# Depthwise convolution in a two-layer backbone step: one tap per channel tile moved from TensorE to VectorE, the first VectorE tap moved to ScalarE, and a later place for the low part of the gated input

## What is computed

```python
def conformer_conv(h, w_pw1, b_pw1, w_dw, b_dw, ln_g, ln_b, w_pw2, b_pw2):
    a = h @ w_pw1 + b_pw1                                  # 1024 -> 2048 channels
    g = a[..., :D_MODEL] * jax.nn.sigmoid(a[..., D_MODEL:])
    y = depthwise_conv(g, w_dw, width 31, padding 15) + b_dw
    y = jax.nn.silu(layer_norm(y, ln_g, ln_b))
    return y @ w_pw2 + b_pw2
```

## Time and profile before

| | |
|---|---|
| Median of three runs | 1706.77 us (1700.06 to 1707.30) |
| The profiled execution, its own time | 1705.06 us |
| Its span in the profile | 1703.1 us |
| TensorE matmuls / VectorE / ScalarE / GpSimd, busy in the whole span | 97% / 56% / 37% / 14% |
| Mean granted TensorE clock | 0.988 of full speed |
| The stretch that the change touches | about 957 to 1144 us in the span |

### The profile page before, as it was taken

How to read it: one execution, slowest core, us unless ns; L and a number is a source line. 1 busy time by engine, 2 the same in 40 slices (tenths; PEclk the granted TensorE clock), 3 DMA queues, 4 the chain that set the end, 5 groups by cost and what they waited for, 6 DMA issues and landing times.

```text
span 1703.1 us, 26511 instructions
## 1 busy us (share of the span) xinstructions
PE 1650.8 (97%) x11277; PEld 1599.8 (94%) x11277; DVE 958.4 (56%) x1617; ACT 636.5 (37%) x988; POOL 242.1 (14%) x288
## 2 busy tenths in 40 slices
PE   8989999989999999999999999999999999999998
PEld 6988778789999999999999999999999999999998
DVE  5556666565774645454458899996663223223222
ACT  3435545453543423342336434354342211221112
POOL 0001111000164523452343000001000000000000
PEclk9999999999999999999999999999999999999999
DMA  8222232142253434433342111010222222221211
GB/s 309 94 68 81 81 94 71 33 137 75 90 164 118 154 97 130 158 125 120 116 124 81 50 50 51 25 50 1 75 77 73 82 67 87 70 89 54 93 56 63
DMA packets 131709, 154.74 MB, mean 91 GB/s; under 512 B 11809, under 2 KB 115177, under 8 KB 131592
## 3 DMA queue, kind: packets, MB, share of 16 engines
q1 hardware_dynamic: 117824, 109.68, 20.4%
q0 software_dynamic: 13440, 43.26, 8.1%
q10 hardware_dynamic: 328, 0.10, 0.0%
HBM read 148.93 MB, written 2.79 MB: 89 GB/s over the span
## 4 chain that ended last, share of the span: by engine, by line
PE 67%; DVE 12%; ACT 2%; issue 2%; POOL 1%; DMA 0%; DVEq 0%; ACTq 0%; POOLq 0%
PE PS L605 21%; PE PS L607 21%; PE PS L610 21%; DVE YACC L2124 7%; PE PS L674 1%; ACT WH L1168 1%; POOL BGACC L582 1%; DVE SUM L1585 1%; PE PS L701 1%; PE PS L927 1%; DVE WL L1577 1%; DVE GP L2103 0%; DVE Y L2133 0%; PE PS L890 0%; DVE Y L2156 0%
## 5 line engine op out<-in xcount | busy, mean ns | idle before, releaser
L605 PE MATMUL PS<-HH,WH 128*128 128x320 f32 x1776 | 412.8, 314 | 11.7 <-DVE HL L1725 4.4
L607 PE MATMUL PS<-HL,WH 128*128 128x320 f32 x1776 | 406.8, 311 | 0.0
L610 PE MATMUL PS<-HH,WL 128*128 128x320 f32 x1776 | 405.7, 310 | 0.0
L1577 DVE TENSOR_TENSOR WL<-RAW,WH 128x2048 fp32r<-128x2048 f32 (+2 forms) x95 | 214.4, 2257 | 204.4 <-ACT WH L1168 203.8
L605 PEld LDWEIGHTS PS<-HH,WH 128*128 128x128 f32 x1776 | 298.0, 190 | 16.0 <-issue 5.7
L607 PEld LDWEIGHTS PS<-HL,WH 128*128 128x128 f32 x1776 | 300.5, 190 | 0.0
L610 PEld LDWEIGHTS PS<-HH,WL 128*128 128x128 f32 x1776 | 300.2, 190 | 0.0
L1168 ACT ACTIVATE WH<-RAW 128x2048 fp32r<-128x2048 f32 (+2 forms) x95 | 171.7, 1807 | 116.6 <-PE PS L610 116.6
L1741 DVE SCALAR_TENSOR_TENSOR X<-PS,MODV,X 128x128 f32<-128x128 f32 (+2 forms) x192 | 72.4, 433 | 206.6 <-PE PS L610 206.6
L582 POOL TENSOR_TENSOR BGACC<-BGACC,BGW 128x512 f32<-128x512 f32 x98 | 134.9, 1376 | 207.1 <-ACT BGW L1423 206.0
L605 PE MATMUL PS<-HIDH,WH 128*128 128x320 f32 x704 | 162.3, 312 | 1.0 <-DVE HIDL L2061 0.7
(11 more groups left out here) (293 smaller groups left out, 2306.4 us busy)
## 6 DMA issues: line engine op xcount, KB each, us to landing
BGW<-in_w_mod POOLq DMA_DIRECT2D x112, 256.0 KB, 3.0
RAW<-in_ffn_w_gate SPq DMA_DIRECT2D x22, 1024.0 KB, 5.3
RAW<-in_ffn_w_up SPq DMA_DIRECT2D x22, 1024.0 KB, 5.3
RAW<-in_ffn_w_down SPq DMA_DIRECT2D x16, 1024.0 KB, 5.1
MODA<-in_w_mod POOLq DMA_DIRECT2D x48, 256.0 KB, 4.0
MODS<-in_w_mod SPq DMA_DIRECT2D x16, 512.0 KB, 12.1
RAW<-in_conv_w_pw SPq DMA_DIRECT2D x16, 512.0 KB, 4.9
RAW<-in_ffn_w_down SPq DMA_DIRECT2D x8, 768.0 KB, 4.4
```

The lines of the kernel that those rows point to most:

```text
L605: mm(o, wh, xh, start=first, stop=False)
L607: mm(o, wh, xl, start=False, stop=False)
L610: ins = mm(o, wl, xh, start=False, stop=last)
L1577: V.tensor_tensor(WL[:, u % 2, 0:n], RAW[:, u % 2, 0:n], WH[:, u % 2, 0:n].bitcast(F32), ALU.subtract).then_inc(lo_done, 1)
```

## The change

The first VectorE tap with the bias becomes a ScalarE instruction behind the GPH copy; tiles 0 to 6 have one tap fewer on TensorE (10, and 12 for tile 6) and so one more off it; tile 7 keeps 18. VectorE waits for ScalarE's tap before its own first one. `gated` no longer has any tap nor GPL in it; GPL is made by `gated_low`, which stands behind all taps of the iteration. `cut` is 19 for tiles 1 to 5 (two taps stand behind `gated(i+1)`), 12 for tile 0 and 8 for tile 6 as before.

```diff
-PE_TAPS = (11, 11, 11, 11, 11, 11, 13, 18)
+PE_TAPS = (10, 10, 10, 10, 10, 10, 12, 18)
...
                 A(GPH[i % 2][:], GP[i % 2][:], ACT.Copy).then_inc(sem("gp_hi"), 1)
+                j = PE_TAPS[i]
+                A(YACC[i % 2][:], GP[i % 2][:, j:j + RUN], ACT.Identity, scale=WTAP[:, i, j:j + 1],
+                  bias=VT2[:, V2["b_dw"] + i:V2["b_dw"] + i + 1]).then_inc(sem("tap_first"), 1)
...
                     was_read(dve, n)
-                first_tap(i)
-                taps(i, 1, 2)
+
+            def gated_low(i):
+
                 dve.wait_ge(sem("gp_hi"), i + 1)
                 V.tensor_tensor(GPL[i % 2][:], GP[i % 2][:], GPH[i % 2][:].bitcast(F32), ALU.subtract).then_inc(sem("gp_lo"), 1)
...
-            def first_tap(i):
-
-                j = PE_TAPS[i]
-                link(V.tensor_scalar(YACC[i % 2][:], GP[i % 2][:, j:j + RUN], WTAP[:, i, j:j + 1],
-                                     VT2[:, V2["b_dw"] + i:V2["b_dw"] + i + 1], ALU.mult, ALU.add))
-
             def taps(i, first, end):
 
                 acc, g = YACC[i % 2], GP[i % 2]
                 j0 = PE_TAPS[i]
+                if first == 1:
+                    dve.wait_ge(sem("tap_first"), i + 1)
                 for j in range(j0 + first, min(j0 + end, TAPS)):
...
             gated(0)
+            gated_low(0)
             for i in range(KT):
                 split_units(U[("glu", i)] + 2)
                 if i:
                     joined(i - 1)
 
-                cut = 8 if i == KT - 2 else 12 if i == 0 else TAPS
-                taps(i, 2, cut)
+                cut = 8 if i == KT - 2 else 12 if i == 0 else TAPS - PE_TAPS[i] - 2
+                taps(i, 1, cut)
                 if i + 1 < KT:
                     gated(i + 1)
                 taps(i, cut, TAPS)
+                if i + 1 < KT:
+                    gated_low(i + 1)
             joined(KT - 1)
```

## The result

The changed kernel took 1715.79 us (median of 8 runs, 1709.47 to 1718.28), the kernel before, run beside it and with its earlier runs, 1704.76 us (8 runs, 1700.06 to 1709.74). The ratio is 1.006 with a 95% interval of 1.0043 to 1.0076: slower by 0.6%. The profiled execution's span is 1713.5 us against 1703.1.

The account below looks back on a forecast made before the run. VectorE was taken to bound the convolution. Its longer tiles, the late GPL(7), 2.3 us of clock loss and 2.84 us of clock holders put the mean +10.45 us later: 1705.06 becomes 1715.5 us, range 1709 to 1719.

Parts of the forecast that it names:

- VectorE sets the pace: Convolution stretch: VectorE's list, 24.56 us a tile before, sets the time, so TensorE's 6.35 us taken away buy nothing.
- The tap on ScalarE: Between ScalarE's copy and rounding: VectorE's low weight part starts 0.72 us later per tile, bounds 0.14 and 0.82.
- The rule that such work belongs on VectorE: Skill's advice against the ScalarE tap, 0.62 us on VectorE against 0.82; by the rule alone 1.6 us in sum.
- TensorE as the most contended engine: Skill's pick by share of weight loads, 94%; the forecast said the chain of the convolution stretch does not agree.
- What a tile costs TensorE: Convolution tile on TensorE: 24.3 us before the change against VectorE's 24.56, then 23.4 against 25.3.
- the rival with TensorE: Convolution: TensorE sets the pace, so the change takes 6.35 us off, 1698.7 us; chance 0.05.
- Late GPL(7): Iteration 6: eleven taps ahead of GPL(7) leave TensorE idle 6.5 to 8 us, so cv(7) ends last.
- The nine taps in tile 0: Tile 0: nine taps ahead of GPL(1); any wait of cv(1) comes out of TensorE's 5 us wait ahead of b(3).
- The clock: At cv(7), behind TensorE's idle time: the granted clock falls and costs 2.3 us, bounds 1.7 and 4.8.
- The clock holders: Behind cv(7): the holders' 2.84 us end last, against VectorE's 1.72 for joining and sum.
- TensorE's waits ahead of b(i+1): Each tile: TensorE waits nearly 2 us (1 to 2) for the gated input, about 5 us in tile 2.
- All behind the mean moves with it: Behind the mean: one dependent chain, shifted by the same +10.45 us as the mean.

Follow-up runs that it names:

- e4_taps_only: Kernel before with only the changed kernel's tap shares, one tap per tile from TensorE to VectorE in tiles 0 to 6: 1713.06 us, ratio 1.0048.
- e5_first_tap_only: Changed kernel with the old tap shares, ScalarE's first tap behind the weight unit's rounding, GPL two taps behind the gated input in every tile: 1696.82 us, ratio 0.9956.
- e1_low_early: Changed kernel with GPL of tile 7 made two taps behind its gated input instead of eleven: 1711.33 us, ratio 1.003.
- e2_hold_cv7: Changed kernel with 26 more matmuls without use ahead of TensorE's wait for GPL(7), to keep the clock up: 1710.09 us, ratio 1.0035.
- e6_no_holders: Changed kernel without the 12 clock holders ahead of the mean: 1717.36 us, ratio 1.0076 to the kernel before.
- e9_tile7_19: e5_first_tap_only with 19 instead of 18 taps of tile 7 on TensorE: 1698.73 us, ratio 0.9969 to the kernel before.
- e8_scalar_tap_first: e5_first_tap_only with ScalarE's tap ahead of the rounding, as in the changed kernel: 1704.60 us, ratio 1.0002 to the kernel before.

## Why the prediction was right

The forecast was 1715.5 us, slower by more than 0.5%; measured were 1715.79 and a ratio of 1.006. Step by step, all counted from the start of the first gated input:

| step | forecast | measured |
|---|---|---|
| gated(1) | 16.95 | 17.06 |
| gated(2) | 47.25 | 47.37 |
| gated(6) | 148.40 | 148.95 |
| gated(7) | 163.40 | 164.04 |
| start of GPL(7) | 174.87 | 175.52 |
| start of cv(7) | 175.8 | 176.50 |
| cv(7) longer by the clock | 2.3 | 2.43 |
| the mean | 197.3 | 197.94 |

- **VectorE sets the pace:** shown by e4_taps_only, where TensorE's 6.35 us bought nothing and VectorE's 6.55 were paid in full.
- **The tap on ScalarE:** its mechanism was right, its size somewhat off. I took 0.72 us from the rows of Identity with a bias; the tap takes 0.92 us in itself (0.82 estimated) and 0.83 from start to start, just past my upper bound of 0.82. Six rounding waits at 0.11 more are the 0.64 by which gated(7) came later. The new instruction has a scale from memory beside the bias, which those rows lacked; whether this makes the 0.10 was not tried.
- **The rule that such work belongs on VectorE** (the Trainium skill, "ScalarE: Activation LUTs", Rules for kernel authors): e5_first_tap_only measured 4.79 us of gain for the opposite. The instruction is indeed longer on ScalarE, 0.92 against 0.62 us, and that costs nothing where that engine is idle and nobody waits behind it.
- **TensorE as the most contended engine** (the Trainium skill, "Perfetto Trace Analysis", Identifying the Most-Contended Engine), at 94% by weight loads: in this stretch not so, by e4_taps_only.
- **What a tile costs TensorE:** counted too high. The working from the end gave 24.3 us before the change; from the start of one tile's convolution to the next it is 24.05 to 24.07 us in tiles 3 to 5. The margin to VectorE's 24.56 was 0.5 us and not 0.24, which makes the rival with TensorE weaker and changes no term of the sum.
- **Late GPL(7):** right, 4.57 us by e1_low_early, the clock's share in it. The nine taps in tile 0 made TensorE wait 1.27 us ahead of cv(1), inside its time to spare, as forecast. The idle time of 6.62 us lies at the lower end of my 6.5 to 8, as the clock had fallen ahead of b(7).
- **The clock:** 2.3 forecast, 2.43 measured, 2.35 by e2_hold_cv7. The size was borrowed from another stretch, so that it came this near is partly luck.
- **The clock holders:** they do end last, but by 0.45 us (e6_no_holders); the forecast's 2.84 against 1.72 made it 1.12.
- **TensorE's waits ahead of b(i+1):** 4.57 us in tile 2 (about 5 forecast), then 0.43, 1.98, 0.43, 1.99 where I had 1 to 2 in each. They alternate. Behind 1.98 the clock fell and the slow matmuls used up most of the next wait; behind 0.43 it stayed up. The five stretches behind the waits of 4.57, 0.43, 1.98, 0.43 and 1.99 us, in order:

```profile
1003.70:1008.50 4.80, 4.79 (x22) 4.79 (x23) 4.04 (x4) 4.80 (x9) 0.00 (x0) 0.64 0.02 3
1029.10:1033.50 4.40, 4.39 (x30) 4.39 (x31) 3.64 (x4) 4.40 (x7) 0.00 (x0) 1.00 0.01 2
1054.50:1059.00 4.50, 4.50 (x20) 4.50 (x21) 3.74 (x4) 4.50 (x8) 0.00 (x0) 0.62 0.00 0
1079.90:1084.50 4.60, 4.60 (x31) 4.60 (x32) 3.83 (x4) 4.60 (x8) 0.00 (x0) 1.00 0.00 0
1105.30:1110.00 4.70, 4.70 (x21) 4.70 (x22) 3.94 (x4) 4.70 (x8) 0.00 (x0) 0.64 0.00 0
```

- **"All behind the mean moves with it"** was wrong by 1.73 us in the profiled run. The sum is close partly by chance: the span of the profiled execution grew by 10.4 us, which is +11.08 in M, +1.73 behind it, and -2.33 for a first gated input that came earlier, within what it moves by between like kernels. Up to the mean the forecast had +10.45 us where 11.08 were measured.

## What to carry to other kernels

Ask who waits for the next instruction on the helping engine. Work moved onto an idle engine is free only behind the things that others wait for: here the same ScalarE instruction cost all it saved ahead of the rounding, and won 4.8 us behind it. When a producer step moves behind other work, check it in each iteration of the loop, the irregular last ones above all: two taps behind it were harmless in five tiles, eleven in one tile cost 4.6 us.

## What the runs showed of the hardware that was not expected

The stretch of light work behind the mean (single-column matmuls, clock holders, small VectorE steps) has a length of 22.77 us in e5_first_tap_only, 24.98 before, 26.71 in the changed kernel and 26.81 in e9_tile7_19, with the same instructions. It goes with the granted clock: over all eleven profiles it is 22.77 us at a mean clock of 0.93, 24.98 to 25.34 at 0.80, and 26.02 to 26.81 at 0.74 to 0.76. These are that stretch before, then in e5_first_tap_only, then in e9_tile7_19 (PEclk 0.80, 0.93 and 0.75):

```profile
1144.30:1169.30 25.00, 22.79 (x150) 22.11 (x151) 12.12 (x33) 8.88 (x13) 6.12 (x4) 0.80 0.00 1
```

```profile
1140.40:1163.20 22.80, 19.83 (x151) 18.97 (x151) 12.14 (x33) 8.94 (x13) 6.13 (x4) 0.93 0.00 1
```

```profile
1137.40:1164.20 26.80, 24.41 (x151) 23.74 (x151) 12.10 (x33) 8.91 (x13) 6.12 (x4) 0.75 0.00 1
```

In the changed kernel the clock stayed at its lower level for 13.6 us on end here, though TensorE was busy all the time:

```profile
1161.00:1174.60 13.60, 13.60 (x65) 13.60 (x66) 3.26 (x18) 1.56 (x3) 3.07 (x2) 0.50 0.00 1
```

The other surprise is that the length of an idle time of about 2 us does not tell whether the clock falls behind it. In e4_taps_only TensorE stood for 2.08 us ahead of b(5) and 2.09 ahead of b(6); behind the first the clock stayed up, behind the second it fell:

```profile
1056.60:1061.00 4.40, 4.40 (x30) 4.40 (x31) 4.18 (x4) 4.40 (x9) 0.00 (x0) 1.00 0.00 0
1082.10:1086.50 4.40, 4.39 (x21) 4.39 (x22) 4.18 (x4) 4.40 (x9) 0.00 (x0) 0.67 0.00 0
```

In e6_no_holders it stood for 1.98 us ahead of b(5) and 1.98 again ahead of b(7); behind the first the clock fell, behind the second it stayed up:

```profile
1057.70:1062.30 4.60, 4.60 (x21) 4.60 (x22) 3.84 (x4) 4.60 (x8) 0.00 (x0) 0.63 0.00 0
1108.50:1113.00 4.50, 4.50 (x31) 4.50 (x31) 3.73 (x4) 4.50 (x8) 0.00 (x0) 1.00 0.01 4
```

In e8_scalar_tap_first it stayed up even behind 2.37 us ahead of b(3) (1.00 over the next 8.7 us), where it had fallen behind 2.47 us in the kernel before. What else decides it, no run here shows.

Back to the stretch behind the mean: up to 4 us of a kernel's time hang on the clock in a stretch that no edit touched. What decides when it falls there was not tried.
